# Small loads on ScalarE's queue, one product for a modulation row, and a Fourier layer whose root is applied behind the transform

## The chip, the cores and the metric

One Trainium2 chip, one of its cores. The metric is device time in microseconds (us) of one execution of the program, lower is better. A median of three runs is given, and beside it the profile of one execution more.

## The reference, cut to what matters

The model works on 256 tokens `x` and 256 context tokens `ctx` of width 1024. A first block has two layers, a second block two more. Each layer of the first block is a half feed-forward step, a mixer (Fourier in the first layer, retention in the second), and another half feed-forward step; before each of the three stands a norm whose gain and shift come from a condition vector:

```python
silu_c, silu_cc = silu(c), silu(c_ctx)
m_lat = split((silu_c @ ada_w[l] + ada_b[l])[:, None, :], 9)      # nine modulation rows of 1024
m_ctx = split(silu_cc @ ada_w[l] + ada_b[l], 9)
rmsnorm(x, g) = x * rsqrt(mean(x * x, axis=-1) + eps) * g          # the root is one number per token
modulate(h, shift, scale) = h * (1 + scale) + shift
h_lat = modulate(rmsnorm(x, norm_g[l, 1]), m_lat[3], m_lat[4])     # the same for ctx with m_ctx

def fourier_mix(h):                                                # 4 groups of 256 channels
    hg = h.reshape(b, n, 4, 256)
    return fft2(hg, axes=(1, 3), norm="ortho").real.reshape(b, n, d)
y = fourier_mix(h) @ four_w + four_b
x = x + m_lat[5] * y
```

All is float32. The second block (attention and a gated linear scan) is not touched by the change.

## The kernel before, in words

The residual stream `x` lies channel by channel: `x[:, k, :]` is chunk k of 128 channels (DC = 8 chunks), with 512 columns, 256 of x and then 256 of ctx. Every linear layer is a stream of weight slots. A slot is one column block of 128 outputs; four slots (SLOTS) are in flight, slot s in bank s. SyncE loads a slot's weights to `raw[s]` (L626), ScalarE rounds them to `whi` (`split_hi`, L1199), VectorE subtracts to get `wlo` (`split_lo`, L1537), and TensorE multiplies in three products per chunk: L672, L673, L674 in `block_mm` (`whi` by the high part of the input, `whi` by its low part, `wlo` by the high part). `mm_done[s]`, `bank_free[s]`, `hi_done[s]`, `lo_done[s]` are the semaphores of a slot. `phases` names the layers in order: `a00gu0` is the gate and up projection of the first half of feed-forward a00, `a00dn1` the down projection of its second half, then `four`, `a01gu0` and so on. With 512 columns and 8 chunks a slot takes TensorE 5.4 us.

**The start.** SyncE issues sixteen small loads (the identity; fourteen vectors into `rows`, c and c_ctx among them; `lg`) and then the 512 KB pieces of `ada_w` for the first two modulation rows (`ada_first`), with x and ctx after the fifth. TensorE waits for all small loads, turns the three tiles of `rows` (L789 to L791), VectorE copies them to `vec` (L1631), ScalarE takes the Silu of c and c_ctx (L1235), VectorE puts them into `first_cs`, and TensorE runs the sixteen `first_unit`s (L799, two products of 512 columns each; five of them, then the turning of x at L812, then eleven).

**The other sixteen modulation rows.** VectorE adds up `ada_w[k] * silu(c)[k]` over the chunks during the feed-forward slots (`ada_unit`), turns the sum in blocks of 32x32 and reduces it to `ada_group` (`group_row`), 128 partitions x 2 streams x 32. Partition 32q + c holds part of the sum for output c of the blocks; what is left is a sum over the four partition groups q and a sorting of the 32 columns into partitions. TensorE does it with four products in the middle of a slot, between the chunks (`ada_reduce(j)`, L694): each takes the stationary matrix `group_sel[:, 3-j:7-j]`, zero but for one block, and the 16 columns of block j. VectorE then adds the bias and the gain (`finish_row`, L1583).

**The norm.** `do_norm` on GpSimd sums squares of chunks 0 to 6, ScalarE squares chunk 7 (`take_squares`, L1252), TensorE sums over partitions in bank 4 (`root_sum`, L829), ScalarE takes the root (`take_root`, L1259), VectorE its reciprocal `rstd` (L1688), one number per token with the tokens in partitions. TensorE spreads it to bank 7 over all partitions (`root_spread`, L854); VectorE multiplies x by gain and spread root (L1711) and ScalarE adds the shift (L1288 in the Fourier case, into `t_full`). `fill(n)` (L818) issues n products whose result nobody reads, around these waits.

**The Fourier layer.** Stage one turns each 128-token tile of each group of 256 channels into half its frequencies: 16 units i = 4g + m, each of two products with 258 columns (L915), into banks 4, 5, 6 in turn; a unit's bank is emptied to `four_a` by ScalarE (m = 0, 1; `take_dft`, L1267) or VectorE (m = 2, 3; L1789). In stage one the tokens are in the output's partitions. Stage two is 16 steps j of four products with 129 columns (L928) over the tokens, into banks 4 to 7; ScalarE copies the sine half to `four_q` (L1323), VectorE adds and subtracts the halves (L1801, L1802), and both split the result for the layer `four`.

A float32 product is recorded as two weight loads and two products.

## Time and profile before

| what | value |
|---|---|
| median of 3 runs | 3257.28 us (3257.18 to 3257.92) |
| the profiled execution, its own time | 3256.22 us |
| its span in the trace | 3254.4 us |
| TensorE busy | 3221.7 us, 99% |
| VectorE, ScalarE, GpSimd busy | 2377.1, 1312.8, 611.5 us (73%, 40%, 19%) |
| mean granted TensorE clock | 0.998 of full speed |
| DMA | 507.58 MB, mean 156 GB/s |

The profile is of one execution. Its own time is the span and 1.8 us around it. In the profile PE is TensorE, PEld its weight loads, DVE VectorE, ACT ScalarE, POOL GpSimd and SP SyncE (SPq is the engine's queue of issued loads); L672 is line 672 of the kernel, and "<-" in brackets names what ended an engine's idle time. A product's recorded time is longer than the step to the next one, since products overlap; what a product costs is read from start to start.

### The profile page before, as it was taken

The page shows a single profiled execution, that of the slowest core. Times are in us where ns is not written, and L with a number is a line of the kernel's source. Part 1 is how long each engine was busy: PE and PEld are TensorE (multiplying, and loading weights), DVE is VectorE, ACT ScalarE, POOL GpSimd, SP SyncE. Part 2 cuts the span into 40 slices and gives each one's busy share as a digit, 9 for nine tenths or more (in the row PEclk, how much of TensorE's full clock was granted, in tenths as well). Part 3 has the DMA queues.
Part 4 walks back from the last instruction along what each step waited for, and adds up shares of the span by engine and source line. Part 5 has one row for each costly group of instructions (what it writes and reads, how often), then busy time and mean ns, then how long its engine had stood idle before and what let it go on. Part 6 is the DMA issues. An engine that isn't in the chain of part 4 may idle for free.

```text
span 3254.4 us, 48129 instructions
## 1 busy us (share of the span) xinstructions
PE 3221.7 (99%) x18145; PEld 2793.3 (86%) x18145; DVE 2377.1 (73%) x3031; ACT 1312.8 (40%) x1757; POOL 611.5 (19%) x514
## 2 busy tenths in 40 slices
PE   8999999999999999999999999999999999999999
PEld 4888888888888888888888899989888889989988
DVE  4877856868777635455768887966888896875887
ACT  3222233212232123333536455355645545446643
POOL 2212322202321121001323230000223231000122
PEclk9999999999999999999999999999999999999999
DMA  6655514646365432334665665444666665443665
GB/s 223 205 158 169 161 48 137 199 138 188 101 187 176 136 104 85 104 100 140 196 180 161 197 183 154 129 130 140 184 191 178 195 190 161 128 130 113 194 197 149
DMA packets 820515, 507.58 MB, mean 156 GB/s; under 512 B 15093, under 2 KB 786225, under 8 KB 820337
## 3 DMA queue, kind: packets, MB, share of 16 engines
q1 hardware_dynamic: 819968, 503.74, 52.6%
q8 instruction: 123, 2.02, 0.2%
q0 software_dynamic: 368, 1.38, 0.1%
q14 instruction: 56, 0.45, 0.0%
HBM read 504.01 MB, written 1.05 MB: 155 GB/s over the span
## 4 chain that ended last, share of the span: by engine, by line
PE 57%; DVE 3%; ACT 0%; issue 0%; DVEq 0%; ACTq 0%
PE bank L670 17%; PE bank L668 10%; PE bank L672 5%; PE bank L673 5%; PE bank L674 5%; PE bank L667 2%; PE bank L687 2%; PE bank L689 2%; PE bank L688 2%; PE bank L1132 2%; DVE wlo_all L1537 1%; PE bank L990 1%; PE bank L1046 1%; PE bank L1051 1%; PE bank L957 0%; DVE xn_two L1627 0%
## 5 line engine op out<-in xcount | busy, mean ns | idle before, releaser
L1537 DVE TENSOR_TENSOR wlo_all<-raw,whi_all 128x1024 fp32r<-128x1024 f32 (+3 forms) x768 | 1005.8, 1312 | 470.5 <-ACT whi_all L1199 467.4
L1199 ACT CAST whi_all<-raw 128x1024 fp32r<-128x1024 f32 (+3 forms) x768 | 834.2, 1090 | 1127.7 <-PE bank L674 676.0
L672 PE MATMUL bank<-xn_two,whi_all 128*128 128x512 f32 (+1 forms) x2144 | 748.7, 349 | 3.4 <-DVE xn_two L1703 3.2
L674 PE MATMUL bank<-xn_two,wlo_all 128*128 128x512 f32 (+1 forms) x2144 | 732.3, 342 | 0.0
L673 PE MATMUL bank<-xn_two,whi_all 128*128 128x512 f32 (+1 forms) x2144 | 732.3, 342 | 0.0
L670 PE MATMUL bank<-xn_two,whi_all 128*128 128x512 f32 x1540 | 550.5, 397 | 0.0
L668 PE MATMUL bank<-xn_two,wlo_all 128*128 128x256 f32 x1760 | 456.4, 280 | 1.0 <-DVE xn_two L1703 0.8
L2178 POOL CAST h_two<-silu_g 128x256 f32 (+1 forms) x176 | 202.7, 1152 | 1340.1 <-DVE silu_g L1769 770.3
L672 PEld LDWEIGHTS bank<-xn_two,whi_all 128*128 128x128 f32 x2144 | 406.3, 189 | 50.1 <-issue 4.5
L674 PEld LDWEIGHTS bank<-xn_two,wlo_all 128*128 128x128 f32 x2144 | 405.9, 189 | 46.5
L673 PEld LDWEIGHTS bank<-xn_two,whi_all 128*128 128x128 f32 x2144 | 406.3, 190 | 45.6 <-issue 0.7
L668 PEld LDWEIGHTS bank<-xn_two,wlo_all 128*128 128x128 f32 x1760 | 332.6, 189 | 22.5 <-DVE xn_two L1703 3.2
L670 PEld LDWEIGHTS bank<-xn_two,whi_all 128*128 128x128 f32 x1540 | 289.7, 188 | 59.6
L670 PE MATMUL bank<-h_two,whi_all 128*128 128x512 f32 x800 | 284.5, 397 | 0.0
L668 PE MATMUL bank<-h_two,wlo_all 128*128 128x256 f32 x880 | 233.0, 280 | 0.0
L2180 POOL TENSOR_TENSOR h_two<-silu_g,h_two 128x256 f32 (+1 forms) x176 | 224.4, 1275 | 32.5 <-POOL h_two L2178 32.5
L672 PE MATMUL bank<-h_two,whi_all 128*128 128x512 f32 x528 | 206.1, 390 | 0.0
L674 PE MATMUL bank<-h_two,wlo_all 128*128 128x512 f32 x528 | 205.5, 389 | 0.0
L673 PE MATMUL bank<-h_two,whi_all 128*128 128x512 f32 x528 | 205.4, 389 | 0.0
L1547 DVE SCALAR_TENSOR_TENSOR ada_acc<-ada_w,sil_c,ada_acc 128x1024 f32<-128x1024 f32 x112 | 183.0, 1634 | 0.8
L670 PEld LDWEIGHTS bank<-h_two,whi_all 128*128 128x128 f32 x800 | 150.3, 188 | 32.7
L668 PEld LDWEIGHTS bank<-h_two,wlo_all 128*128 128x128 f32 x880 | 165.9, 189 | 7.1
(322 smaller groups left out, 4570.3 us busy)
## 6 DMA issues: line engine op xcount, KB each, us to landing
raw<-in_ffn_w_in SPq DMA_DIRECT2D x176, 512.0 KB, 3.8
raw<-in_w_in SPq DMA_DIRECT2D x168, 512.0 KB, 3.8
ada_w<-in_ada_w SPq DMA_DIRECT2D x128, 512.0 KB, 4.1
raw<-in_ffn_w_gate SPq DMA_DIRECT2D x88, 512.0 KB, 3.9
raw<-in_ffn_w_up SPq DMA_DIRECT2D x88, 512.0 KB, 4.0
raw<-in_ffn_w_down SPq DMA_DIRECT2D x32, 768.0 KB, 5.1
raw<-in_ret_w_in SPq DMA_DIRECT2D x48, 512.0 KB, 3.8
raw<-in_ffn_w_out SPq DMA_DIRECT2D x32, 768.0 KB, 4.8
```

What stands on the lines that cost most here:

```text
L667: pe.matmul(both, whi[s][:, k, :], two, start=True, stop=False)
L668: mm = pe.matmul(o, wlo[s][:, k, :], hi, start=False, stop=False)
L670: mm = pe.matmul(both, whi[s][:, k, :], two, start=False, stop=(k == ks - 1))
L672: pe.matmul(o, whi[s][:, k, :], hi, start=(k == 0), stop=False)
L673: pe.matmul(o, whi[s][:, k, :], lo, start=False, stop=False)
L674: return pe.matmul(o, wlo[s][:, k, :], hi, start=False, stop=(k == ks - 1))
L687: pe.matmul(bank[b][:], hi[:, k, c], w_hi, start=(k == 0), stop=False)
L1199: act.copy(whi[s][:, 0:ks, :], raw[s][:, 0:ks, :]).then_inc(hi_done[s], 1)
L1537: tt(wlo[s][:, 0:ks, :], raw[s][:, 0:ks, :], whi[s][:, 0:ks, :].bitcast(F32), ALU.subtract).then_inc(lo_done[s], 1)
L1547: stt(ada_acc[0][:], w[:], sil_c[:, k, 0:1], ada_acc[0][:], ALU.mult, ALU.add).then_inc(ada_sum, 1)
L2178: pool.tensor_copy(hi[:, ds(2 * it + p, 1), 0:T], full).then_inc(h_rounded[p], 1)
L2180: tt(lo[:, ds(2 * it + p, 1), 0:T], full, hi[:, ds(2 * it + p, 1), 0:T].bitcast(F32), ALU.subtract).then_inc(h_done[p], 1)
```

## The change

1. Small loads go to ScalarE's queue. First only the identity, c and c_ctx (into a small tile of their own, `cond_rows`) are loaded and turned; Silu reads them from PSUM. The other fourteen vectors and `lg` follow, and TensorE turns them after the first five units. SyncE starts with `ada_first`.
2. `ada_reduce` is one product with 64 columns: the stationary matrix repeats the sum over partition groups four times, so every partition gets all blocks, and VectorE's addition of the bias picks the right columns in four operations of 32 partitions.
3. The Fourier layer's norm has no spreading. The input of stage one is x times the gain alone (`four_x`, written by ScalarE behind the slots of `a00dn1`), the root `rstd` is multiplied in when a unit's bank is emptied, since tokens lie in partitions there. The shift, the same for all tokens, touches only frequency 0 of the tokens: its transform is four small products (`shift_sums`), written to column 0 of `four_q`, which now holds all 16 steps. Stage one uses six banks instead of three; the column sums of the norm go to bank 7 behind the third unit. The fillers of this norm go.

```diff
 # norm and order of the layer (planner)
-        a = norm(2 * SEQ, None, (l, 1), "plain" if l == 0 else "split")
+        a = norm(2 * SEQ, None, (l, 1), "fourier" if l == 0 else "split")
 # TensorE
-            def ada_reduce(j):
-                mm = pe.matmul(bank[5][:, 0:2 * DC].rearrange("p (k s) -> p k s", s=2),
-                               group_sel[:, 3 - j:7 - j, :].rearrange("p a b -> p (a b)"),
-                               ada_group[:].rearrange("p s (k j) -> p k s j", j=4)[:, :, :, j],
-                               start=(j == 0), stop=(j == 3))
-                if j == 3:
-                    mm.then_inc(ada_cols, 1)
+            def ada_reduce():
+                pe.matmul(bank[5][:, 0:64], group_sel[:].rearrange("p a b -> p (a b)"),
+                          ada_group[:].rearrange("p s c -> p (s c)"), start=True, stop=True).then_inc(ada_cols, 1)
...
-                            if row and 1 <= k < 5:
-                                ada_reduce(k - 1)
+                            if row and k == 1:
+                                ada_reduce()
...
-            pe.wait_ge(in_sem, 16 * n_inputs)
-            (the three turning products of `rows` into bank 4)
-            pe.wait_ge(vec_ready, 1)
+            pe.wait_ge(in_sem, 16 * n_cond)
+            pe.transpose(bank[7][:, 0:2 * DC], cond_rows[0:2 * DC, :], ident[0:2 * DC, 0:2 * DC]).then_inc(vec_t, 1)
             pe.wait_ge(first_c, 1)
...
             for j, k in first_order[:FIRST_AHEAD]:
                 first_unit(j, k)
+            pe.wait_ge(in_sem, 16 * n_inputs)
+            (the same three turning products, into bank 7)
             pe.wait_ge(x_landed, 32)
             for k in range(DC):
+                if k == 3:
+                    pe.wait_ge(vec_ready, 1)
...
 # do_fourier on TensorE
+        FOUR_BANKS = (4, 0, 1, 2, 3, 6)
+                def shift_sums():
+                    pe.wait_ge(rstd_done, a["norm"]["n"] + 1)
+                    shift = mod[:, 0, 3].rearrange("p (g c) s -> p c g s", c=2)
+                    for lc in range(2):
+                        for c in range(2):
+                            mm = pe.matmul(bank[5][:, 8 * lc:8 * lc + 8].rearrange("p (g s) -> p g s", s=2),
+                                           dft[:, c, lc * P:(lc + 1) * P], shift[:, c], start=(c == 0), stop=(c == 1))
+                    mm.then_inc(f_b, 1)
                 for g in range(4):
                     pe.wait_ge(plain, 4 * (g + 1))
                     for m in range(4):
                         i = 4 * g + m
-                        if i >= 3:
-                            pe.wait_ge(*dft_taken(i - 3))
+                        if i >= 6:
+                            pe.wait_ge(*dft_taken(i - 6))
+                        elif 1 <= i <= 4:
+                            pe.wait_ge(bank_free[i - 1], r0 + 1)
                         (two products: t_full -> four_x, bank[4 + i % 3] -> dft_bank(i))
+                        if i == 2:
+                            root_sum(a["norm"])
+                        if i == 8:
+                            shift_sums()
-                pe.wait_ge(f_ae, 8)
-                pe.wait_ge(f_aed, 8)
                 for j in range(16):
+                    if lc == 0:
+                        pe.wait_ge(*dft_taken(4 * g + 2 * st + 1))
+                    if j < 3:
+                        pe.wait_ge(*dft_taken((12, 10, 11)[j]))
 # ScalarE
+            act.dma_start(ident[:], const["ident"]).then_inc(in_sem, 16)
+            for i, src in enumerate((A["c"][0], A["c_ctx"])):
+                act.dma_start(cond_rows[DC * i:DC * i + DC, :], src.rearrange("(r p) -> r p", p=P)).then_inc(in_sem, 16)
+            act.wait_ge(vec_t, 1)
+            act.activation(sil_c[:, :, 0], bank[7][:, 0:DC], ACT.Silu)
+            act.activation(sil_c[:, :, 1], bank[7][:, DC:2 * DC], ACT.Silu).then_inc(silc, 1)
+            (the fourteen loads into `rows` and that of `lg`, moved here from SyncE)
             act.wait_ge(vec_ready, 1)
...
+            def scaled(a, k):
+                act.wait_ge(*chunk_ready(a["src"], k))
+                for st in range(2):
+                    c = slice(st * SEQ, (st + 1) * SEQ)
+                    act.activation(four_x[:, k, c], x[:, k, c], ACT.Copy, scale=mod[:, 0, 4, k, st:st + 1])\
+                        .then_inc(plain, 1)
...
 # ScalarE, do_norm: take_squares; scaled(a, DC - 1); take_root; in a00dn1, behind split_hi: scaled(a, k), k = 0 to 6
 # ScalarE, take_dft
-                        e = act.copy(four_a[:, i % 4, g, lc, :, :], half[:, :, dft_rows(lc)])
+                        e = act.activation(four_a[:, i % 4, g, lc, :, :], dft_bank(i)[:, :, dft_rows(lc)], ACT.Copy,
+                                           scale=rstd[:, i % 4:i % 4 + 1])
 # ScalarE, do_fourier
+                act.wait_ge(rstd_done, a["norm"]["n"] + 1)
+                for g in range(3):
+                    take_dft(g)
+                act.wait_ge(f_b, 1)
+                (two activations: shift sums, times -16 and 16, to column 0 of the 16 steps in four_q; f_ae)
                 take_dft(3)
...
-                    act.copy(four_q[:, j % 4, :], bank[4 + j % 4][:, SEQ:SEQ + 129]).then_inc(f_q, 1)
+                    act.copy(four_q[:, j, 1:129], bank[4 + j % 4][:, SEQ + 1:SEQ + 129]).then_inc(f_q, 1)
 # VectorE
-                            finish_row(l, j, bank[5][:, 0:2 * DC].rearrange("p (k s) -> p k s", s=2))
+                            sums = bank[5][:, 0:64].rearrange("p (s k q) -> p k s q", s=2, q=4)
+                            for q in range(4):
+                                parts = slice(32 * q, 32 * q + 32)
+                                add_bias(l, j, parts, sums[parts, :, :, q])
+                            finish_row(l, j)
...
+                dve.wait_ge(rstd_done, a["norm"]["n"] + 1)
...
-                            e = dve.tensor_copy(four_a[:, i % 4, g, lc, :, :], half[:, :, dft_rows(lc)])
+                            e = tsc(four_a[:, i % 4, g, lc, :, :], dft_bank(i)[:, :, dft_rows(lc)],
+                                    rstd[:, i % 4:i % 4 + 1], None, ALU.mult)
```

## Rows read from the trace of the kernel before

**Rows 1.** The page, part 1: busy us, share of the span, instructions.
```profile
PE 3221.7 (99%) x18145; PEld 2793.3 (86%) x18145; DVE 2377.1 (73%) x3031; ACT 1312.8 (40%) x1757; POOL 611.5 (19%) x514
```

**Rows 2.** Who TensorE waited for, 55 to 1160 us: us in total, times, longest.
```profile
PE bank L829 <- ACT silu_g L1252: 2.1, 3, 1.2
...
PE bank L672 <- DVE xn_two L1703: 0.8, 1, 0.8
```

**Rows 3.** Timeline of the start: start us, us, instruction, [idle before <-releaser].
```profile
0.75 0.35 SPq L591 DMA_DIRECT2D ident<-const_ident  x1
...
6.72 0.36 SPq L606 DMA_DIRECT2D lg<-in_ret_decay  x1
7.12 2.63 SPq L612 DMA_DIRECT2D ada_first<-in_ada_w  x5
...
9.55 0.47 PE L789 MATMUL bank<-ident,rows 128*128 128x128 f32 x1 [9.55 <-DMA lg<-in_ret_decay]
...
10.17 0.36 PE L791 MATMUL bank<-ident,rows 60*128 60x60 f32 x1
...
10.56 0.49 DVE L1631 COPY vec<-bank 128x316 f32<-128x316 f32 x1 [10.56 <-PE bank L791]
...
11.09 0.21 ACT L1235 ACTIVATE sil_c<-vec 128x8 f32<-128x8 f32 x1 [9.05 <-DVE vec L1631]
...
11.86 11.06 PE L799 MATMUL bank<-ada_first,first_cs 128*4 128x512 f32 x20 [1.33 <-DVE first_cs L1638]
```

**Rows 4.** The same timeline, TensorE's turning of x and the units after it.
```profile
22.84 3.89 PE L812 MATMUL bank<-ident,tok_in 128*128 128x128 f32 x32
...
26.66 17.33 PE L799 MATMUL bank<-ada_first,first_cs 128*4 128x512 f32 x40
```

**Rows 5.** One tile, ada_first: time from the issue of its loads to their landing.
```profile
DMA to landing us min/median/max: 4.1/13.4/15.1
```

**Rows 6.** One tile, ada_group: duration ns min/median/max, first and last start us.
```profile
L694 PE MATMUL bank<-ada_group,group_sel x128: 191/229/263, 129.6 to 1133.8; 128*128 128x16 f32 x128
```

**Rows 7.** Timeline of TensorE in a slot with `ada_reduce`.
```profile
407.32 0.39 PE L673 MATMUL bank<-h_two,whi_all 128*128 128x512 f32 x1
...
410.26 0.40 PE L674 MATMUL bank<-h_two,wlo_all 128*128 128x512 f32 x1
410.50 0.29 PE L694 MATMUL bank<-ada_group,group_sel 128*128 128x16 f32 x2
...
411.18 0.39 PE L674 MATMUL bank<-h_two,wlo_all 128*128 128x512 f32 x1
```

**Rows 8.** One source line, VectorE's addition of a bias row.
```profile
L1583 DVE TENSOR_TENSOR mod<-bank,vec x18: 160/167/174, 49.4 to 1139.4; 128x16 f32<-128x16 f32 x18
```

**Rows 9.** Timeline of TensorE from the down projection's end through both transforms.
```profile
417.58 1.50 PE L818 MATMUL bank<-ident 128*128 128x128 f32 x12
419.50 0.35 PE L829 MATMUL bank<-ones,sumsq 128*128 128x1 f32 x2 [0.42 <-ACT silu_g L1252]
...
421.28 0.92 PE L818 MATMUL bank<-ident 128*128 128x128 f32 x6
...
426.46 14.09 PE L915 MATMUL bank<-dft,t_full 128*128 128x258 f32 x64
441.49 14.53 PE L928 MATMUL bank<-dft,four_a 128*128 128x129 f32 x128 [0.94 <-DVE four_a L1789]
```

**Rows 10.** Timeline of ScalarE around the Fourier norm.
```profile
410.01 1.05 ACT L1199 CAST whi_all<-raw 128x1024 fp32r<-128x1024 f32 x1 [5.75 <-PE bank L674]
...
419.37 1.28 ACT L1259 ACT_TABLE_LOAD   x1
```

**Rows 11.** Timeline of VectorE around the Fourier layer.
```profile
421.82 0.18 DVE L1688 RECIPROCAL rstd<-rstd 128x4 f32<-128x4 f32 x1 [1.45 <-ACT rstd L1259]
...
461.54 1.00 DVE L1811 TENSOR_SCALAR t_full<-bank,vec,mod 128x256 f32<-128x256 f32 x2 [3.80 <-PE bank L674]
```

**Rows 12.** One stretch: length, busy us by engine, PEclk, DMA, GB/s.
```profile
422.00:426.50 4.50, 4.50 (x27) 4.45 (x26) 2.93 (x8) 2.42 (x7) 0.00 (x0) 0.62 0.26 77
```

More of the change, by code:

```diff
@@ L806, in _ @@
                 first_unit(j, k)
+            pe.wait_ge(in_sem, 16 * n_inputs)
+            pe.transpose(bank[7][:, 0:P], rows[:, 0, :], ident[:])
+            pe.transpose(bank[7][:, P:2 * P], rows[:, 1, :], ident[:])
+            pe.transpose(bank[7][:, 2 * P:2 * P + VEC3], rows[0:VEC3, 2, :], ident[0:VEC3, 0:VEC3]).then_inc(vec_t, 1)
             pe.wait_ge(x_landed, 32)
             for k in range(DC):
+                if k == 3:
+                    pe.wait_ge(vec_ready, 1)
                 if k >= 4:
@@ L822, in root_sum @@
                 tiles = a["T"] // P
-                if a["n"]:
+                if a["n"] and a["mode"] != "fourier":
                     fill(2 + tiles)
@@ L828, in root_sum @@
                     for n, part in enumerate((sumsq, silu_g[0])):
-                        mm = pe.matmul(bank[4][:, c:c + 1], part[:, c * P:(c + 1) * P], ones[:, 0:1], start=(n == 0),
-                                       stop=(n == 1))
+                        mm = pe.matmul(stat_bank(a)[:, c:c + 1], part[:, c * P:(c + 1) * P], ones[:, 0:1],
+                                       start=(n == 0), stop=(n == 1))
                 mm.then_inc(stat, 1)
@@ L874, in do_norm @@
             def do_norm(a):
-                if a["n"] and not a["late"]:
+                if a["n"] and not a["late"] and a["mode"] != "fourier":
                     root_sum(a)
@@ L905, in do_fourier @@
             def do_fourier(a):
+                r0 = phases["four"]["first"]
                 pe.wait_ge(trig_landed, 48)
+                def shift_sums():
[6 more added lines that the diff above has]
+                    mm.then_inc(f_b, 1)
                 for g in range(4):
@@ L1313, in do_ffn @@
                         lower_bounds()
-                    stream(f"{a['tag']}dn{half}")
-            def do_fourier(a):
+                    name, behind = f"{a['tag']}dn{half}", None
+                    for kind, b in steps:
+                        if kind == "norm" and b["mode"] == "fourier" and b["src"] == name:
+                            behind = lambda it, s, b=b: SLOTS * it + s < DC - 1 and scaled(b, SLOTS * it + s)
+                    stream(name, behind=behind)
+            def do_fourier(a):
+                act.wait_ge(rstd_done, a["norm"]["n"] + 1)
+                for g in range(3):
+                    take_dft(g)
+                act.wait_ge(f_b, 1)
+                zero = four_q[:].rearrange("p (g l s) f -> p l g s f", l=2, s=2)
+                for lc in range(2):
+                    i = act.activation(zero[:, lc, :, :, 0], bank[5][:, 8 * lc:8 * lc + 8].rearrange("p (g s) -> p g s", s=2),
+                                       ACT.Copy, scale=(-16.0, 16.0)[lc])
+                i.then_inc(f_ae, 1)
                 take_dft(3)
                 def sines(j):
-                    act.wait_ge(f_b, j + 1)
-                    if j >= 4:
-                        act.wait_ge(f_y, j - 3)
-                    act.copy(four_q[:, j % 4, :], bank[4 + j % 4][:, SEQ:SEQ + 129]).then_inc(f_q, 1)
+                    act.wait_ge(f_b, j + 2)
+                    act.copy(four_q[:, j, 1:129], bank[4 + j % 4][:, SEQ + 1:SEQ + 129]).then_inc(f_q, 1)
                 sines(0)
@@ L1577, in group_row, with add_bias, finish_row @@
                 i.then_inc(ada_grouped, 1)
-            def finish_row(l, j, cols):
+            def add_bias(l, j, parts, cols):
+                bias = vec[parts, (V_AB0, V_AB1)[l] + DC * j:(V_AB0, V_AB1)[l] + DC * (j + 1)]
+                n = parts.stop - parts.start
+                link(tt(mod[parts, l, j], cols, bias.unsqueeze(2).broadcast_to([n, DC, 2]), ALU.add))
+            def finish_row(l, j):
                 row = mod[:, l, j]
-                bias = vec[:, (V_AB0, V_AB1)[l] + DC * j:(V_AB0, V_AB1)[l] + DC * (j + 1)]
-                link(tt(row, cols, bias.unsqueeze(2).broadcast_to([P, DC, 2]), ALU.add))
                 link.after()
@@ L1628, in gained_low @@
                     ALU.subtract).then_inc(xn, 1)
-            dve.wait_ge(vec_t, 1)
-            dve.tensor_copy(vec[:, 0:2 * P + VEC3], bank[4][:, 0:2 * P + VEC3]).then_inc(vec_ready, 1)
             for s in (2, 3):
@@ L1638, in _ @@
             dve.tensor_copy(first_cs[:, 1, :, 2:4], sil_c[:]).then_inc(first_c, 1)
[L1639 removed]
+            link(dve.tensor_reduce(group_one[:], ident[:].rearrange("p (q c) -> p c q", q=4), AXX, ALU.add))
             link.after()
[L1641 to L1642 removed]
+            dve.tensor_copy(group_sel[:], group_one[:].unsqueeze(1).broadcast_to([P, 4, 32])).then_inc(sel_ready, 1)
+            dve.wait_ge(vec_t, 2)
+            dve.tensor_copy(vec[:, 0:2 * P + VEC3], bank[7][:, 0:2 * P + VEC3]).then_inc(vec_ready, 1)
             for k in range(DC):
@@ L1711, in do_norm @@
                         stt(t[:, k, c], x[:, k, c], g, root[:, c], ALU.mult, ALU.mult).then_inc(t_done, 1)
-                    if k and a["mode"] != "plain":
+                    if k:
                         low(k - 1)
-                if a["mode"] != "plain":
-                    low(DC - 1)
+                low(DC - 1)
             def residual(xt, s, k, T, gate):
```

106 lines of the change are left out of this document (52 added, 54 removed).

## The prediction

> **What bounds the kernel now.** I read the page's busy times first. TensorE is busy for 3221.7 of 3254.4 us [rows 1], and the reader is to see from it that only two kinds of edit can pay: fewer TensorE instructions, or a shorter stretch in which TensorE waits or runs filler. The list of who waited for whom says where it waits. From 55 to 1160 us it has three entries, of 2.1 us at most (the first and the last stand in the group), and none is for the split weights `wlo_all` [rows 2]; so VectorE and ScalarE keep ahead there, and work added to them costs nothing while it stays small. The timeline of the start comes next: TensorE does its first product at 9.55 us and its first useful one (`first_unit`) at 11.86 us, and from there runs without a gap into the turning of x at 22.84 [rows 3, 4]. The timeline of the Fourier norm was last: after the down projection there are 8.9 us (417.58 to 426.46) of filler, column sums, spreading and waiting before the first transform product [rows 9].
>
> **Part 1, the small loads.** Before, SyncE issues sixteen small loads from 0.75 to 7.08 us and only then the 512 KB loads of `ada_w`; TensorE waits for all sixteen [rows 3]. After, ScalarE issues three (identity, c, c_ctx), and SyncE begins with `ada_first` at once, 7.12 - 0.75 = 6.4 us earlier. Three issues at about 0.4 us a step (0.75, 1.15, 1.55). The last of the small loads was issued at 6.72 and the products that waited for it began at 9.55, 2.8 us later; so the three have landed at about 1.55 + 2.8 = 4.4. Before, 1.69 us pass from the start of the last turning product (10.17) to the first unit (11.86); the copy to `vec` (10.56 to the Silu at 11.09, 0.53 us) leaves that chain, 1.16 remain, and the first unit starts at 5.6. Its own operand is there: a first load that lands 4.1 us after its issue [rows 5] has landed at 4.9. Gain 11.86 - 5.6 = 6.3 us. The three big turning products, now in front of x's, cost TensorE 3 x 0.12 = 0.4 (32 such products take 3.89 us) [rows 4]. The copy to `vec` then runs under the first 12 turning products of x (1.4 us against 0.5). Net: **5.9 us**. Queued behind ScalarE's wait for `vec_t` are the other fifteen issues, from 5.2 to about 11 us; TensorE asks for them after five units, at 5.6 + 11.0 = 16.6, and ScalarE's next work is the square of x's last chunk, later still. x and ctx need not be looked at again: their loads move ahead by 6.4 us and TensorE by 6.3.
> Bounds: not before 4.9 (the first `ada_first`), a gain of 6.6; if the table load (1.28 us [rows 10]) comes before the three issues and the small packets share with the large ones for 1 us more, 3.6. The first units run slower: 20 records take 11.0 us, where 40 later ones take 17.3 [rows 3, 4], so 8.7 for 20 and 2.4 us lost; that loss can come out 1 us smaller or larger.
> The Trainium skill ("DMA: Bandwidth & Descriptors", Issuing engines are not separate DMA queues) says that loads issued from ScalarE and SyncE run on the same 16 engines and interleave, so a second queue saves issue time alone. By it the sum keeps its 5.9, since that is issue time. Its section Queues, rings and completion order speaks against: a completion is written only after every earlier write of the same DMA engine, across its queues. By that the small loads would be reported late behind large ones; the second rival prices this from rows.
>
> **Part 2, one product for a row.** Sixteen rows of the modulation go through `ada_reduce`: 128 records of the form 128x16 [rows 6], so four products of two records a row. Inside a slot one costs what it pushes the stream back: from one L674 to the next with an `ada_reduce` between are 0.92 us (410.26, 411.18) [rows 7], while three block products alone take 0.68 (the records from 407.32 to 410.26 are 13 steps of 0.226). So 0.24 us each, and 3 x 16 = 48 fewer are **11.5 us**. The one left has 64 columns instead of 16, a form that the trace doesn't show. Two records with one column take 0.22 us (16 of them from 419.50 to 421.28), and two with 128 columns 0.25 (twelve in 1.50) [rows 9]: 64 lies between, so its cost is unchanged within 0.02 each, 0.3 in all; I take 0. If it took a cost of its own on top, up to 0.1, the gain is 9.9; at most it is 12.
> VectorE gets four additions of 32 partitions instead of one of 128, at 0.17 us [rows 8]: 0.5 us a row, 8 us in all. It lies under slots of 5.4 us, and a late split is wanted only three slots on; without that cover it is 8 us. In the last slot before the Fourier norm VectorE has 1.45 us of idle time before the reciprocal [rows 11], which takes the 0.5.
>
> **Part 3, the Fourier layer.** Removed: the fillers (6, 3 and 8 products, two records each, before, between and after), the spreading (8 records), sixteen scalings by VectorE and sixteen shifts by ScalarE. The sixteen new scalings go behind the down projection, where ScalarE sits idle 5.75 us before each cast [rows 10]; only the last chunk's pair runs after 419.4. So the transform of chunks 0 and 1 can start at 417.58. Its order on TensorE: three units, the column sums, thirteen units with the shift sums after the ninth.
> Costs: 16 units x 4 records x 0.217 = 13.9 us (64 in 14.09 with the tail); column sums 1.8 (419.50 to 421.28); shift sums 4 products, 8 records at the one-column step of 0.11, 0.9. Stage two can begin at 417.58 + 16.6 = 434.2, where before it began at 441.49 [rows 9]. **7.3 us**, with the 0.94 us for VectorE's last copy in it: the first product of stage two now needs group 0 and bank 4 only.
> Does anything hold it? Column sums at 417.58 + 3 x 0.87 = 420.2; their square is done at 419.4, where the table load starts [rows 10]. They end at 422.0; before, the reciprocal ended 0.7 us after them (421.28 to 422.00) [rows 9, 11], so `rstd` is there at 422.7. Only then are banks emptied. TensorE wants the first one back for its seventh unit, at 424.6; ScalarE has emptied two by 424.2. A group takes VectorE four operations at 0.50 (its nearest row, a multiply from PSUM with column scalars [rows 11]) = 2.0 us, against TensorE's 3.5. So no stall; if the cover of six banks were too thin, the first to wait is the seventh unit. Stage two itself is unchanged, TensorE at 0.89 us a step and VectorE close behind.
> The clock: in the old gap the granted clock was 0.62 over 4.5 us [rows 12], that is 3.4 us at the lower level, 1.2 GHz. It fell on spreading and fillers. If such a stretch fell on transform products it would take 1.7 us back, a gain of 5.6. The upper bound is 7.5. Other norms can gain or lose such a stretch too: 1.7 us either way.
>
> **Sum.** 5.9 + 11.5 + 7.3 = 24.7 us. The profiled execution took 3256.22 us (its span 3254.4), 1.1 below the median of 3257.28, which is inside what I can resolve. 3256.2 - 24.7 = **3231.5**. The bounds of the three parts give gains from 3.6 - 1 + 9.9 + 5.6 - 1.7 = 16.4 to 6.6 + 1 + 12 + 7.5 + 1.7 = 28.8, but hardly all at one end; its own range is 3228 to 3236.
>
> **The rivals.**
> - *The small loads land late* (chance 0.09). Once `ada_first` loads are queued the median from issue to landing is 13.4 us [rows 5]. If c and c_ctx came in only after five such loads (1.3 us each), the first unit starts near 11.9 and part 1 gives nothing: 3237.4. If the fifteen others took 15.1 us from 11, TensorE would stand from 16.6 to 26 and part 1 costs 3 us: 3240.8. Against it: at 1 us the DMA engines are empty, and the small ones are issued beside the first.
> - *The Fourier layer is held* (0.09): a low clock, or TensorE stands at the column sums or the seventh unit because ScalarE's new scalings push cast, square or root back. The two scalings of the last chunk stand ahead of the root on ScalarE, 0.9 us. From 3233.2 (clock) to 3238.8 (all of part 3 gone).
> - *The row product isn't cheaper* (0.02): one 64-column product costs as four; 3243.0.
> - *Slower* (0.02): the fillers were what kept the clock up. With them gone it falls at the layer's start and stays low. The two transform stages are 28 us of products at the full rate; at the lower level they take 28 more, and with the column and shift sums 31. 3231.5 + 31 = 3262. It decides once more than 24.7 us are lost, that is 49 us at 1.2 GHz. Against it: the same products ran from 426.5 on with no filler among them and no wait longer than 0.94 us.
> - Two of these together, 0.02, about 3243.
> The forecast has 0.76.
>
> **How the numbers follow.** The range of 8 in 10 takes the forecast's own, the mild end of the Fourier rival and the mild end of the late loads: 3227 to 3238. A measurement tells 0.2% (6.5 us) from no change, so slower than 3250.8 counts as the same. Forecast, late loads, held layer and dear product all lie below: 0.96 faster; 0.02 the same, 0.02 slower.
>
> **What the new profile would show.** First `first_unit` product near 5.6 us, and the first block product 6 us earlier than before. 32 records of L694's kind instead of 128, of 64 columns, and 0.24 us each pair. The first transform product right after the last L674 of the down projection, no wait in the list for the transform stages, stage two 16.6 us after stage one. Wrong if TensorE's wait for the identity ends after 6 us, if a wait for `four_a` stands at the seventh unit, or if new waits for `wlo_all` appear between 55 and 1160 us.

## The result and the profile after

The changed kernel takes 3238.36 us in the median of 4 runs (3237.76 to 3239.18), the kernel before on the same chip 3257.6 us: ratio 0.9941, interval 0.9923 to 0.9958, clear of 1. That is 19.2 us less, where 24.7 were forecast, and 0.4 us above the upper end of the range. In the profiled executions the span (first to last instruction) went from 3254.4 to 3236.9, 17.5 us. The profiles show where these 17.5 us came from, so I use them for the sizes, and the medians as the check.

The page of the changed kernel, part 1, against [rows 1]: TensorE's busy time fell by 13.9 us, and VectorE's stayed.
```profile
PE 3207.8 (99%) x18016; PEld 2780.7 (86%) x18016; DVE 2377.2 (73%) x3063; ACT 1314.2 (41%) x1759; POOL 616.6 (19%) x514
```

**The start.** Timeline of the changed kernel, against [rows 3, 4]:
```profile
0.74 0.38 ACTq L1247 DMA_DIRECT2D ident<-const_ident  x1
0.75 2.54 SPq L607 DMA_DIRECT2D ada_first<-in_ada_w  x5
...
1.86 0.28 ACTq L1249 DMA_DIRECT2D cond_rows<-in_c_ctx  x1
...
7.01 0.28 PE L780 MATMUL bank<-ident,cond_rows 16*128 16x16 f32 x1 [7.01 <-DMA cond_rows<-in_c_ctx]
...
7.34 0.31 ACTq L1256 DMA_DIRECT2D rows<-in_ada_b  x1
...
7.99 10.94 PE L787 MATMUL bank<-ada_first,first_cs 128*4 128x512 f32 x20 [0.70 <-DVE first_cs L1701]
...
12.88 0.36 ACTq L1273 DMA_DIRECT2D lg<-in_ret_decay  x1
...
20.40 0.33 PE L796 MATMUL bank<-ident,rows 128*128 128x128 f32 x1 [1.47 <-DMA lg<-in_ret_decay]
...
20.97 3.89 PE L806 MATMUL bank<-ident,tok_in 128*128 128x128 f32 x32
```
The three small loads were in at 7.01, not at 4.4. So the first unit starts at 7.99 instead of 5.6: 3.87 us earlier than before and not 6.3. After the five units TensorE stands 1.47 us for the last of the fifteen others, and the three turnings take 0.57. x is turned at 20.97, before at 22.84: the start gives 1.87 us.

**The rows.** The product's new form, and a slot with it (against [rows 6, 7]):
```profile
L689 PE MATMUL bank<-ada_group,group_sel x32: 217/245/274, 127.7 to 1114.3; 128*128 128x64 f32 x32
```
```profile
405.21 0.39 PE L669 MATMUL bank<-h_two,wlo_all 128*128 128x512 f32 x1
405.44 0.33 PE L689 MATMUL bank<-ada_group,group_sel 128*128 128x64 f32 x2
...
408.21 0.39 PE L669 MATMUL bank<-h_two,wlo_all 128*128 128x512 f32 x1
```
From 405.21 to 408.21 are 3.00 us for twelve block products and the row's: 3.00 - 12 x 0.227 = 0.274 us for it (0.227 is one block product from start to start, here 0.91 / 4 from 404.53 to 405.44). The four of before took 4 x 0.24 = 0.96. Sixteen rows give 16 x 0.686 = 10.98 us. But the list of who TensorE's weight loads waited for, 60 to 1160 us, has an entry that before has not:
```profile
PEld bank L667 <- POOL h_two L2245: 0.7, 2, 0.4
```
Both times it is the start of a down projection (363.1 and 809.7), and the stream is pushed back 0.22 us each. The timeline of VectorE ahead of the first of them shows why:
```profile
353.51 1.49 DVE L1594 TENSOR_TENSOR wlo_all<-raw,whi_all 128x1280 fp32r<-128x1280 f32 x1 [1.31 <-ACT whi_all L1212]
354.92 0.77 DVE L1640 TENSOR_TENSOR mod<-bank,vec 32x16 f32<-32x16 f32 x4
355.78 1.28 DVE L1604 SCALAR_TENSOR_TENSOR ada_acc<-ada_w,sil_c,ada_acc 128x1024 f32<-128x1024 f32 x1
356.98 1.28 DVE L1605 SCALAR_TENSOR_TENSOR ada_acc<-ada_w,sil_c,ada_acc 128x1024 f32<-128x1024 f32 x1
358.29 0.69 DVE L1833 TENSOR_TENSOR silu_g<-silu_g,bank 128x512 f32<-128x512 f32 x1
```
The four additions (0.77 us) and two accumulations stand in front of the product of silu and up, with no idle time between them; GpSimd splits that product into `h_two`, and TensorE asks for it. So the rows give 10.98 - 0.44 = 10.54 us.

**The Fourier layer.** TensorE from the end of the down projection (against [rows 9]):
```profile
411.61 0.39 PE L669 MATMUL bank<-h_two,wlo_all 128*128 128x512 f32 x1
411.84 2.77 PE L923 MATMUL bank<-dft,four_x 128*128 128x258 f32 x12
414.44 0.28 PE L823 MATMUL bank<-ones,sumsq 128*128 128x1 f32 x2
...
416.15 5.47 PE L923 MATMUL bank<-dft,four_x 128*128 128x258 f32 x24
421.45 0.95 PE L910 MATMUL bank<-mod,dft 128*128 128x8 f32 x8
422.26 6.34 PE L923 MATMUL bank<-dft,four_x 128*128 128x258 f32 x28
428.44 14.45 PE L941 MATMUL bank<-dft,four_a 128*128 128x129 f32 x128
```
Nothing waits. Stage two starts 428.44 - 411.84 = 16.6 us after stage one, as worked out; before it was 441.49 - 417.58 = 23.91. ScalarE and VectorE (against [rows 10, 11]) take the root and the first bank in time:
```profile
414.43 1.28 ACT L1297 ACT_TABLE_LOAD   x1
416.32 0.27 ACT L1297 ACTIVATE rstd<-bank,eps 128x4 f32<-128x4 f32 x1 [0.61 <-PE bank L823]
416.90 3.02 ACT L1312 ACTIVATE four_a<-bank,rstd 128x256 f32<-128x256 f32 x8 [0.31 <-DVE rstd L1753]
```
```profile
416.69 0.18 DVE L1753 RECIPROCAL rstd<-rstd 128x4 f32<-128x4 f32 x1 [1.46 <-ACT rstd L1297]
416.90 1.66 DVE L1853 TENSOR_SCALAR four_a<-bank,rstd 128x256 f32<-128x256 f32 x4
```

**The other norms.** The windows of the three next norms, each from the end of TensorE's last block product to the start of the next one. First the kernel before, then the changed one; the last three figures are PEclk, DMA share and GB/s:
```profile
499.42:509.35 9.93, 8.56 (x60) 8.23 (x58) 5.60 (x12) 3.64 (x7) 0.00 (x0) 0.83 0.26 77
874.26:882.53 8.27, 7.01 (x59) 6.62 (x58) 5.13 (x13) 4.83 (x8) 0.00 (x0) 1.00 0.22 64
1245.50:1253.70 8.20, 6.93 (x59) 6.61 (x58) 4.88 (x11) 4.83 (x8) 0.00 (x0) 1.00 0.22 66
```
```profile
486.26:497.38 11.12, 9.89 (x59) 9.72 (x58) 5.79 (x13) 3.64 (x7) 0.00 (x0) 0.69 0.24 70
858.41:867.88 9.47, 8.51 (x59) 8.18 (x58) 5.63 (x16) 4.83 (x8) 0.00 (x0) 0.82 0.18 55
1228.11:1236.31 8.20, 6.94 (x60) 6.61 (x58) 4.87 (x11) 4.83 (x8) 0.00 (x0) 1.00 0.22 66
```
The instructions are the same in both kernels, the granted clock is not. A PEclk of 1.00 is the upper of the two levels, 2.4 GHz; a value between 0.5 and 1 means that part of the window ran at the lower one, 1.2 GHz. At PEclk 1.00 the second norm takes 8.27 us, at 0.82 it takes 9.47: one stretch at 1.2 GHz costs 1.2 us. The changed kernel has two such stretches more in these norms than before, 2.4 us. It is no accident of one execution: in the second take below the same three norms show 0.70, 0.83 and 1.00.

The account: 1.87 + 10.54 + 7.39 - 2.39 = 17.4 of 17.5 us (the Fourier part with 0.08 us by which stage two came out shorter).

### The profile page after: what moved, and what is told of

It is laid out like the page before. It is cut to its first block, busy times and chain, and to the rows that moved or that the text cites. A ratio compares the mean times of both kernels' runs of the same rounds, so it can differ in the third digit from the quotient of the medians.

```text
span 3236.9 us, 47905 instructions
## 1 busy us (share of the span) xinstructions
PE 3207.8 (99%) x18016; PEld 2780.7 (86%) x18016; DVE 2377.2 (73%) x3063; ACT 1314.2 (41%) x1759; POOL 616.6 (19%) x514
## 4 chain that ended last, share of the span: by engine, by line
PE 58%; DVE 3%; ACT 0%; issue 0%; DVEq 0%; ACTq 0%
PE bank L665 18%; PE bank L663 10%; PE bank L667 5%; PE bank L668 5%; PE bank L669 5%; PE bank L662 2%; PE bank L682 2%; PE bank L684 2%; PE bank L683 2%; PE bank L1145 2%; DVE wlo_all L1594 1%; PE bank L1003 1%; PE bank L1059 1%; PE bank L1064 1%; PE bank L970 0%; DVE xn_two L1692 0%
## 5 line engine op out<-in xcount | busy, mean ns | idle before, releaser
L2243 POOL CAST h_two<-silu_g 128x256 f32 (+1 forms) x176 | 210.0, 1193 | 1328.1 <-DVE silu_g L1833 758.3
```

What stands on the lines that cost most here:

```text
L2243: pool.tensor_copy(hi[:, ds(2 * it + p, 1), 0:T], full).then_inc(h_rounded[p], 1)
```

## The experiments

Every kernel below is an edit of the changed one, and each ratio is to the kernel before on its own chip. The first four ran on one chip and can be compared directly; for the others I also give the difference to the kernel before on the same chip, which is 19.2 us for the changed kernel.

**The changed kernel again,** unchanged, to see how far two takes differ.

> The changed kernel as it is, once more. If the stretches of low clock (0.5 of full speed, 3.4 us each) in the two norms at 486 and 858 us belong to this kernel, they stand at the same norms again and the time is 3238.4. If they come and go with the execution, they stand elsewhere, and the profiled time moves by 1.2 us for each.

Measured 3238.63 us (3236.25 to 3240.82), ratio 0.9943 (0.9926 to 0.9959). The three loads were turned at 6.29 us and x at 21.23. The low clock stood at the same norms again (PEclk 0.70 from 486.61 to 497.81, 0.83 from 858.90 to 868.67), so by the test set above the stretches belong to this kernel. Two takes of one kernel differ by 0.7 us in when small loads land, and single runs by 4.6 us. Differences of 1 to 2 us must be read from traces.

**No large load until the three small ones are in.**
```
+ sp.wait_ge(in_sem, 16 * n_cond)      # SyncE, ahead of the first ada_first load
```


> SyncE waits for the three small loads before it issues the 512 KB ones. Theory: the small packets were late because they share the DMA engines with the large ones; alone, c_ctx lands 2.8 us after its issue, at 4.7 instead of 7.0 us. The first unit then waits for its own operand, 4.1 us after 4.7, and starts at 8.8, 0.8 later than in the changed kernel: 3239.2. Rival: ScalarE's queue is slow by itself; the landing stays at 7.0, the first unit starts at 11.1: 3241.5.

Measured 3235.11 us (3234.59 to 3237.57), ratio 0.9931 (0.9914 to 0.9948). Two windows side by side, the stretch from 2 to 4 us, in the changed kernel and in this one (last figures: DMA share and GB/s):
```profile
2.00:4.00 2.00, 0.00 (x0) 0.00 (x0) 0.00 (x0) 1.28 (x1) 0.00 (x0) 1.00 0.95 320
```
```profile
2.00:4.00 2.00, 0.28 (x1) 0.18 (x1) 0.01 (x1) 1.53 (x3) 0.00 (x0) 1.00 0.05 14
```
And TensorE in this kernel:
```profile
3.31 0.28 PE L781 MATMUL bank<-ident,cond_rows 16*128 16x16 f32 x1 [3.31 <-DMA cond_rows<-in_c_ctx]
7.43 11.43 PE L788 MATMUL bank<-ada_first,first_cs 128*4 128x512 f32 x20 [3.83 <-DMA ada_first<-in_ada_w]
```
On nearly empty DMA engines the loads are in at 3.31 us, 1.47 after the last issue (1.84); beside the 512 KB loads of the other queue they are in at 7.01, or 5.15 after it (6.29 and 4.43 in the second take). That is the step of my sum that failed, shown by taking the load away. The packets of ScalarE's queue (q10; packets, MB, share) show what was late. First the changed kernel from 5 to 6.5 us, then this one from 2.5 to 3 us:
```profile
q10 hardware_dynamic: 16, 0.00, 1.2%
```
```profile
q10 hardware_dynamic: 16, 0.00, 3.4%
```
Eight of the sixteen carry 512 bytes, together the 4 KB of the last load, and eight carry 4 bytes, which I take for its completion. In the changed kernel the eight of data start between 5.10 and 5.85 us and the last small one at 6.39; with the large loads held back it is 2.73 to 2.94 and 2.97. So of the 3.7 us between the two landings, 2.9 are the data's own lateness. The completion then trails the data by 0.5 instead of 0.03 us, and the product follows it by 0.6 instead of 0.3. The first unit is only a little earlier (7.43), since it now waits for its own operand. The fifteen others, issued from about 3.6, are in when the five units end, and the wait of 1.47 us is gone. The median is 3.5 us below that of the second take, where 0.8 more than the changed kernel was expected: the first unit came at 7.43 and not at 8.8, and the end of that wait was not in the expectation. x is turned at 19.36 instead of 21.23, which is 1.9 of the 3.5; the rest is not explained.

**Five of the fifteen other issues ahead of the wait.** The other ten stay behind it.
```
- act.dma_start(...).then_inc(in_sem, 16)      # identity, c, c_ctx
+ act.dma_start(...).then_inc(cond_sem, 16)
  ... five of the fifteen other issues moved here; ten stay behind the wait ...
  act.wait_ge(vec_t, 1)
```


> Five of the fifteen issues go ahead of ScalarE's wait for the turning product, on a semaphore of their own count. Theory: TensorE's 1.47 us wait for the last small load comes from issues that queue behind that wait; the last is issued 1.8 us earlier, lands before TensorE asks at 18.9, and 1.4 us are gained: 3237.0. Rival: those loads are late because the large ones fill the DMA engines, whenever they are issued; the wait of 1.47 stays: 3238.4.

Measured 3234.75 us (3233.67 to 3237.5), ratio 0.9932 (0.9915 to 0.9948). The three loads still land at 6.33, but no wait stands behind the five units (7.31 to 17.52), and x is turned at 18.09, 3.1 us earlier than in the second take: 2.1 from the wait, 1.0 because the five units took 10.28 us instead of 11.32. The last issue is at 10.29 instead of 12.07. Its landing is no faster: its last packet starts 6.6 us after the issue (16.90), against 7.2 in the changed kernel (12.88 to 20.04). So the wait of 1.47 us (2.07 in the second take) had two causes together: issues queued behind ScalarE's wait for `vec_t`, and a landing of 7 us. Taking away a part of the first was enough; with a landing of 2.8 us there would have been no wait either (12.88 + 2.8 = 15.7, and TensorE asks at 18.9).

**The three loads at the head of SyncE's queue,** and the fifteen others as in the last one.
```
+ for i, src in enumerate((A["c"][0], A["c_ctx"])): sp.dma_start(...).then_inc(cond_sem, 16)
+ sp.dma_start(ident[:], const["ident"]).then_inc(cond_sem, 16)
  for n, (j, k) in enumerate(first_order): ...
```


> As the split issues, and c, c_ctx and identity head SyncE's queue in front of the large loads, while ScalarE issues only small ones. Theory of sharing: c and c_ctx meet few large packets, all three have landed by 4.8, and the first unit starts at 6.1, when its own operand lands: 1.9 us more than the split issues, 3235.1. Rival (landing is set by something else, such as the number of small loads in flight): the turning product stays at 7 us, 3237.0.

Measured 3234.94 us (3234.28 to 3236.11), ratio 0.9932 (0.9915 to 0.9948).
```profile
3.46 0.28 PE L784 MATMUL bank<-ident,cond_rows 16*128 16x16 f32 x1 [3.46 <-DMA ident<-const_ident]
6.20 11.54 PE L791 MATMUL bank<-ada_first,first_cs 128*4 128x512 f32 x20 [2.46 <-DMA ada_first<-in_ada_w]
```
Ahead of the large loads on their own queue, the small ones are in at 3.46 and delay them little: the first unit starts at 6.20, 1.1 us earlier than in the last experiment. But the five units end no earlier, since they take 11.54 us and not 10.28. The first records of this phase stand 0.85 us apart and the later ones 0.43, and here more of them were slow; the warmed start below is about it. So the expected 3235.1 us was met by luck: it counted 1.9 us less than the last experiment, which had been expected at 3237.0 and was already at 3234.75.

**The rows as before,** all else changed: four products of 16 columns, one addition.

> The changed kernel with the modulation rows as before: four 16-column products and one addition of VectorE for a row, instead of one 64-column product and four additions. The prediction puts 11.5 us on this part: about 3249.9 us. The trace of the changed kernel says less: 16 rows x (0.960 - 0.274) = 10.98 us less the two waits of 0.22 us at the start of a down projection, so about 10.5 us and 3248.9 us; the two down projections start 3.00 us after the last gate/up product again, without a wait of TensorE for h_two. Rival: the four additions and the waits have nothing to do with each other (GpSimd is late for another reason); then both waits of 0.22 us stay.

Measured 3247.33 us (3245.1 to 3250.98), ratio 0.9965 (0.9951 to 0.9979): 9.0 us more than the changed kernel (8.7 more than its second take); against the kernel before it is 11.0 us less, so the rows count for 19.2 - 11.0 = 8.2. From the first block product to the start of the Fourier layer it takes 364.93 us, against 361.04: 3.89 more, and the sum says 6 x 0.686 for six rows less 0.22 for the wait, 3.90. The medians give 1.5 to 2.3 us less than the 10.5 expected; the interval of this ratio alone is 4.6 us either way. The entry for `h_two` is gone from the list.

**One addition of VectorE instead of four.**
```
- for q in range(4): add_bias(l, j, parts, sums[parts, :, :, q])
+ add_bias(l, j, slice(0, P), sums[:, :, :, 0])
```


> The changed kernel with one addition of VectorE for a modulation row instead of four; it takes the sums of the first partition group alone, so three quarters of the row's values are left wrong. The 64-column product stays. Theory: the two waits of 0.22 us at the start of a down projection come from the four additions (four of 0.17 to 0.2 us instead of one) ahead of the product of silu(gate) and up; with one addition both waits are gone and a row still costs TensorE 0.27 us: the time falls by 0.4 us beside the place of the low clock stretches. Rival: the waits come from the product's new shape or from elsewhere; then both stay.

This kernel leaves out three quarters of each row's values, and ran once: 3237.51 us, too little to judge a time by. In its trace the 64-column product stays and the entry for `h_two` is gone, which separates the two: the waits came from the additions. VectorE ahead of the same down projection:
```profile
356.51 0.17 DVE L1640 TENSOR_TENSOR mod<-bank,vec 128x16 f32<-128x16 f32 x1
356.77 1.28 DVE L1604 SCALAR_TENSOR_TENSOR ada_acc<-ada_w,sil_c,ada_acc 128x1024 f32<-128x1024 f32 x1
```

**The start as before,** all else changed.

> The changed kernel with the start of before: all sixteen small loads on SyncE's queue, one wait, three turnings, Silu from the turned vector. By the prediction the start is worth 5.9 us: about 3244.3 us. By the trace of the changed kernel it is worth 1.9 us: about 3240.2 us, with the first block product near 52.7 us instead of 50.8 us.

Measured 3238.22 us (3236.58 to 3239.25), ratio 0.9936 (0.992 to 0.9953). The median is not above that of the changed kernel, where by the trace 1.9 us were due. In the profile x is turned at 22.32 us and the first block product comes at 52.16, 1.4 and 1.0 later than in the two takes of the changed kernel; but the first of its three norms took 9.55 us instead of 11.12. A start worth 1 to 2 us and a clock stretch of 1.2 are of one size, and no interval here tells them apart, so the 1.87 us rests on traces alone. What it does settle is that the start is not worth 5.9.

**The Fourier part alone,** on the start and rows of before.

> The kernel before with only the Fourier layer of the change (root behind the transform, raw state transformed, six banks). By the prediction 7.3 us less than before, 3250.0 us. If the parts add up, start_undone and rows_undone give the same for it. Rival: the place of the rare low clock stretches moves the total by some 1.2 us each, so 3248.8 to 3251.2 us.

Measured 3248.55 us (3247.22 to 3251.85), ratio 0.9972 (0.9961 to 0.9984): 9.8 us less than before in the medians, 7.8 in the profiled spans, and in the layer itself 38.20 us become 30.81: 7.39 less. That confirms the layer's 7.39 in a second kernel; the medians carry 2.4 us more that the layer does not explain.

**No products of the identity in the norms.**
```
  def fill(n):
-     for _ in range(n):
-         pe.matmul(bank[6][:, 0:P], ident[:], ident[:], start=True, stop=True)
+     return
```


> The changed kernel without the products of the identity with itself that TensorE does while it waits in a norm; they enter no output. Theory: they keep the granted clock up through the norm gaps, so without them the low stretches (two or three now, some 1.2 us each in their gaps) come in more of the norms, up to one per gap of about 8 us, and the time goes up by 1 to 15 us. Rival: the stretches come whatever is in the gaps, or the fillers themselves stand in the way of the sums; then the time stays within 1 us or falls.

Measured 3247.32 us (3245.82 to 3248.59), ratio 0.9963 (0.9949 to 0.9977): 9.0 us more than with them (8.2 by the differences to the kernel before). The three norms in this kernel:
```profile
489.07:499.72 10.65, 4.88 (x25) 4.39 (x25) 5.59 (x12) 3.64 (x7) 0.00 (x0) 0.67 0.25 74
862.35:872.64 10.29, 5.26 (x26) 4.79 (x25) 5.65 (x16) 4.83 (x8) 0.00 (x0) 0.62 0.17 51
1235.64:1244.55 8.91, 3.95 (x25) 3.47 (x25) 4.87 (x11) 4.83 (x8) 0.00 (x0) 0.76 0.19 59
```
The clock is low in all three, and goes on being low into the block products behind them. The fillers do hold it up, and what they don't prevent are, in the changed kernel, three stretches (two of them in the first norm).

**More of them.**
```
- fill(2 + tiles)
+ fill(2 + tiles + (4 if a["n"] == 2 else 2))
- fill(2 * (a["T"] // P))
+ fill(2 * (a["T"] // P) + 3)
```


> The changed kernel with more products of the identity with itself in the norm gaps: two more in front of the sums (four in the norm behind the Fourier layer, where TensorE waited 1.23 us), three more behind the spread. They enter no output. Theory: the low clock stretches of the norms (gaps of 11.1 and 9.5 us instead of 9 and 8.2) come because TensorE rests in front of the one-column sums; with the rests filled they are gone, and the time is 2.4 us less than that of the changed kernel. Rival: the stretches come from the one-column sums themselves, and stay; then the time is the same or up to 1 us more, where the added products stand in front of the sums.

Measured 3236.65 us (3233.84 to 3239.36), ratio 0.9932 (0.9915 to 0.9948), 1.7 us less in the median (2.6 by the differences to the kernel before), which the intervals don't tell from nothing. In its profile all three norms ran at full clock:
```profile
487.36:496.37 9.01, 8.50 (x73) 8.16 (x72) 5.59 (x12) 3.65 (x7) 0.00 (x0) 1.00 0.30 88
857.40:865.67 8.27, 8.09 (x69) 7.74 (x68) 5.64 (x16) 4.83 (x8) 0.00 (x0) 1.00 0.23 65
1225.92:1234.12 8.20, 8.03 (x69) 7.72 (x68) 4.87 (x11) 4.83 (x8) 0.00 (x0) 1.00 0.20 64
```
The norms took 3.3 us less than in the changed kernel, yet the span is only 0.6 shorter. Part of it went at the start: TensorE stood 3.05 us for the small loads here, then turned x at PEclk 0.51 (20.0 to 23.4 us) in 4.82 instead of 3.89 us. A later stretch, from 1726.7 us, lasted 6.8 us (PEclk 0.50) where the changed kernel's lasts 3.4 (0.51 from 1729.3). And the last kernel, with the same fillers, has a low stretch in two of the three again. So one profile is no proof here, and the cause of the single stretches stays open.

**A warmed start.** The edit of the three loads above (five of the fifteen other issues ahead of the wait, not all of them as the expectation says), and ten products of ones with ones.
```
+ pe.wait_ge(ones_set, 1)
+ warm(4)                                # four products into bank 6, never read
  pe.wait_ge(cond_sem, 16 * n_cond)
  ... turning of c and c_ctx ...
+ warm(6)
```


> The changed kernel with all small issues ahead of any wait, the three small loads of the condition at the head of SyncE's queue, and ten products of a tile of ones with itself ahead of the first unit (four before the three loads have landed, six behind the turning); they enter no output. Theory: the first five units took 10.3 to 11.5 us because their first products ran at the low clock (1.06 us for one of 512 columns instead of 0.59); warmed, they take about 8.6 us from 6.2, and x is turned at 15 to 15.5 us instead of 18.2: some 2.5 to 3 us less than without (3234.9), about 3232. Rival: the operands of the units are then the bound (the second to fifth land 1.3 us apart or later), or ten products do not bring the clock up; then the gain is under 1 us.

Measured 3235.51 us (3233.77 to 3237.05), ratio 0.993 (0.9913 to 0.9947): no gain in the median over 3234.94 (0.5 us by the differences to the kernel before).
```profile
3.64 2.93 PE L786 MATMUL bank<-ones 128*128 128x128 f32 x12
6.50 10.26 PE L799 MATMUL bank<-ada_first,first_cs 128*4 128x512 f32 x20
...
17.68 3.89 PE L818 MATMUL bank<-ident,tok_in 128*128 128x128 f32 x32 [0.35 <-DMA tok_in<-in_ctx]
```
The fillers themselves ran at half rate (twelve records in 2.93 us; in the norm at 486 us twelve take 1.50) and six of them ended 0.3 us too late. The five units take 10.3 us instead of 11.5, and then ctx is not there yet. Neither theory was quite right: full rate does come sooner, and then the load of ctx is the bound, so that the turning starts at 17.68 and not at 15.

**All of it,** with five fillers in place of six behind the turning, and the additions of the two rows in question one slot later. Here too five of the fifteen other issues stand ahead of the wait.
```
+ ends = {g + (u[1:3] in ((0, 6), (1, 3))): u for g, u in ends.items()}
```


> All the remedies at once: small issues ahead of any wait and the condition's three loads at the head of SyncE's queue, nine products of ones to warm the clock, more products in the norm gaps, and the additions of the two rows that end right before a down projection moved one slot back on VectorE. Theory: against the warmed kernel (3235.5, profiled span 3233.5) the norm gaps go from 10.6, 8.9 and 9.1 to 9.0, 8.3 and 8.2 us (3.1 less), and both waits of TensorE for h_two are gone (0.4 less): 3232.0 in the median, ratio to before near 0.992. Rival: low clock stretches come at other places instead (x turning, the last layers), and the median stays at 3234 to 3236.

Measured 3231.59 us (3230.58 to 3234.52), ratio 0.992 (0.9907 to 0.9934), the fastest of the study: 26.6 us less than before, where the changed kernel is 19.2 less. The profiled execution was the slowest of the five. Its span, 3232.7, is 4.2 below that of the changed kernel: 3.3 up to the first block product (47.50 instead of 50.80), 0.44 from the two waits (the entry for `h_two` is gone), 0.5 from the norms. The expected 3232.0 came out, but not by all of its reasons: two norms had a low stretch after all.
```profile
482.71:493.28 10.57, 10.07 (x73) 9.74 (x72) 5.59 (x12) 3.65 (x7) 0.00 (x0) 0.84 0.25 73
854.05:863.53 9.48, 9.48 (x69) 9.28 (x68) 6.51 (x18) 5.42 (x10) 0.00 (x0) 0.82 0.20 57
```

## Why the prediction was wrong, point by point

- **What bounds the kernel:** right. Only work of TensorE, and gaps in it, moved the time.
- **The start, 5.9 forecast, 1.87 measured:** this step failed, in two places. "Three have landed at about 1.55 + 2.8 = 4.4" took the landing time from a load that stood ahead of all large ones on one queue, issued at 6.72 us with the DMA engines' share at 0.08 (6 to 7 us), 0.03 (7 to 8) and only then 0.68 (8 to 9), and used it for loads beside which 512 KB loads would fill them (share 0.95 from 2 to 4 us). My bound for sharing was 1 us; the loads came 2.6 late (7.01 instead of 4.4; 0.3 of it because the third issue was at 1.86 and not at 1.55), and 3.7 against the quiet engines of the experiment. I had argued that at 1 us the DMA engines are empty. They are, but what counts is what they do until the landing. The step cost 2.4 us. The Trainium skill ("DMA: Bandwidth & Descriptors", Queues, rings and completion order) says that a completion comes only behind all earlier writes of that DMA engine, across queues; the order of the times agrees (7.01, against 3.31 and 3.46 where no large load was ahead), but by the packets that rule is the smaller part: the last load's data were themselves 2.9 us late, and the completion trailed them by 0.5. Waiting of the small packets beside the large ones is the main cause. I had made late landing a rival of 0.09 instead of a term of the sum. (That rival's price for the fifteen others, a wait from 16.6 to 26, makes part 1 cost 9.4 - 5.9 = 3.5 us and not 3.)
- The second place: "the other fifteen issues, from 5.2 to about 11 us" was noted and dropped, since TensorE would ask at 16.6. They ran from 7.34 to 13.24, TensorE asked at about 18.9 and got the last at 20.4, so 1.47 us. From its issue (12.88) the last took 7.5 us instead of 2.8 until the product could start, by the same error. The turnings took 0.57 instead of 0.4.
- **The rows, 11.5 forecast, 10.54 measured:** mechanism right, size off by 8%. The 64-column product costs 0.274 us, 0.03 over the 0.24 of the 16-column one, outside my bound of 0.02 (16 x 0.03 = 0.5), and VectorE's additions were not covered in two of sixteen rows (0.44). "Work added to them costs nothing while it stays small" was read from a list of waits over 1100 us. It doesn't hold in the slots ahead of a down projection, where VectorE's product is the next thing TensorE needs.
- **The Fourier layer, 7.3 forecast, 7.39 measured:** right in every step: the start behind the last block product, the sums behind three units, 16.6 us to stage two, no wait.
- **The clock:** forecast at nothing with 1.7 us either way; it cost 2.4. Each of two norms had one stretch more, 1.2 us each, and again in the second take. The experiments show that products in the gaps hold the clock up (8 to 9 us for all of them); why a given norm gets a stretch stays open.
- **Rivals:** the late loads were the true one, at a milder size than I priced. The one by which the Fourier layer's fillers kept the clock up did not come: its transforms ran at full rate from the first product.

From 24.7: less 4.0 (start), less 0.96 (rows), plus 0.09 (Fourier), less 2.4 (clock) is 17.4.

## What to carry to other kernels

A landing time holds only for the load on the DMA engines under which it was measured: when an edit lets large loads start beside small ones that are awaited, take the time from a row with large loads in flight, or put the small ones at the head of the large ones' queue. Behind a wait on an issuing engine, list the issues that queue there, with issue and landing priced anew. And "VectorE has slack" is a statement about an average; look at the slots in which its result is the next thing that TensorE needs.

## What was not expected of the hardware

The small loads on ScalarE's queue were in 5.2 us after the last of their issues beside large loads on SyncE's queue (4.4 in the second take), and 1.5 us after it alone. TensorE's first units run at half rate, 0.85 us a record and not 0.43, which fits 1.2 GHz, though the profile's PEclk column shows 1.00 there. That 1.00 is no reading: the trace has no clock record before 12.43 us in the changed kernel, 16.54 in the one before, 11.85 with the three loads on SyncE's queue and 9.58 in the warmed one, and in each the rate doubles at that record. With ten filler products from 1.0 us on it came 2.3 us earlier (11.85 to 9.58) and this phase took 1.3 us less; that this is their doing is not shown, since the kernel with five issues moved took 10.28 us for the phase without any. And three norms with nearly the same instructions ran at PEclk 0.69, 0.82 and 1.00, at the same places in two takes, which moves a run by 1.2 us a stretch.
